# Projecting blocks 0 and 1 of a hybrid attention and expert layer one at a time, with new pacing marks

## What is computed

```python
h = rms_norm(x, norm1_w)
proj = einsum('bsd,dc->bsc', h, w_in)          # 3592 columns: q,k,v (8 heads of 64), conv q,k,v (4 of 128), gate, a, b
# group A: stick-breaking attention, a block of 128 queries against all earlier keys
# group B: causal conv of width 4 + silu, then a gated delta net whose state runs from block to block
mix = concatenate([o_sb, o_gdn]);  x = x + mix @ w_out
# PEER: for every token 8 heads x 16 experts out of 16384
q = (hn @ w_q); s1, s2 = scores against two sets of 128 sub keys; top 16 of each, top 16 of the sums -> experts, gates
act = gelu(einsum('thkd,td->thk', u_table[experts], hn)) * gates
out = x + einsum('thk,thkd->td', act, v_table[experts])
```

## Time and profile before

| | us |
|---|---|
| median of 3 runs | 3555.86 |
| lowest, highest | 3548.87, 3561.72 |
| the profiled execution, its own time | 3561.24 |
| its span, first to last instruction | 3559.5 |

### The profile page before, as it was taken

How to read it: one execution, slowest core, us unless ns; L and a number is a source line. 1 busy time by engine, 2 the same in 40 slices (tenths; PEclk the granted TensorE clock), 3 DMA queues, 4 the chain that set the end, 5 groups by cost and what they waited for, 6 DMA issues and landing times.

```text
span 3559.5 us, 46354 instructions
## 1 busy us (share of the span) xinstructions
PE 2354.7 (66%) x16193; PEld 1425.5 (40%) x16193; DVE 2318.2 (65%) x5421; ACT 849.8 (24%) x2344; POOL 2308.0 (65%) x2091
## 2 busy tenths in 40 slices
PE   7663546885847759767848859758847784344477
PEld 6543424653524436534524536534514451000011
DVE  3436887776697597666698587667696658444400
ACT  3330012331213223313114123314103311111122
POOL 1001775555667777677777677577687768777775
PEclk9887657897868879878869879878858885555555
DMA  7542899998989999999999999999999999999999
GB/s 233 190 169 97 312 356 328 351 374 301 349 321 357 410 373 411 412 381 390 409 374 387 409 384 410 368 389 395 406 371 369 407 409 346 387 409 409 409 403 374
DMA packets 398905, 1276.24 MB, mean 359 GB/s; under 512 B 44302, under 2 KB 99667, under 8 KB 389459
## 3 DMA queue, kind: packets, MB, share of 16 engines
q0 software_dynamic: 294912, 1073.87, 78.2%
q1 hardware_dynamic: 85330, 157.45, 12.2%
q10 hardware_dynamic: 18432, 41.95, 3.2%
HBM read 1232.18 MB, written 40.93 MB: 358 GB/s over the span
## 4 chain that ended last, share of the span: by engine, by line
POOL 25%; PE 24%; DVE 18%; DMA 17%; issue 9%; ACT 3%; DVEq 3%; ACTq 1%; SPq 0%; POOLq 0%
PE zz L1489 14%; POOL u_ring L684 13%; POOL v_ring L699 11%; DMA v_ring<-in_peer_v,idxT 9%; DVE u_ring L1067 5%; PE va L1489 4%; PE rr L1489 4%; DMA u_ring<-in_peer_u,idx 4%; DMA u_ring<-in_peer_v,idxT 2%; PE ox L1489 1%; DMA work<-d_w 1%; POOL u_ring L699 1%; DVE work L1398 1%; DVE work L1400 1%; DMA work<-d_gv 1%
## 5 line engine op out<-in xcount | busy, mean ns | idle before, releaser
L684 POOL DMA_INDIRECT u_ring<-in_peer_u,idx x1024 | 1177.2, 1150 | 786.4 <-DVE work L1414 330.3
L1067 DVE SCALAR_TENSOR_TENSOR u_ring<-u_ring,hn_t 128x1024 f32<-128x1024 f32 x1024 | 1223.1, 1222 | 387.2 <-DMA u_ring<-in_peer_u,idx 383.6
L699 POOL DMA_INDIRECT v_ring<-in_peer_v,idxT x960 | 1061.5, 1106 | 422.2 <-issue 248.6
L1489 PE MATMUL va<-v_ring,column 128*32 128x256 f32 x7680 | 748.3, 493 | 618.3 <-DMA v_ring<-in_peer_v,idxT 562.8
L1489 PE MATMUL zz<-work 128*128 128x256 f32 (+3 forms) x3232 | 739.0, 390 | 62.4 <-DVE work L1248 12.6
L1489 PEld LDWEIGHTS zz<-work 128*128 128x128 f32 (+1 forms) x3232 | 552.6, 212 | 270.7 <-issue 136.6
L1489 PEld LDWEIGHTS va<-v_ring,column 128*32 128x32 f32 x7680 | 196.9, 124 | 1096.9 <-DMA v_ring<-in_peer_v,idxT 888.0
L763 ACT ACTIVATE column<-onehot,wT 128x32 f32<-128x32 f32 x1024 | 285.9, 315 | 805.7 <-PE va L1489 777.5
L1489 PE MATMUL zz<-work,w_q_t 128*128 128x128 f32 x1024 | 132.0, 292 | 1.8 <-DVE work L1314 1.8
L1489 PEld LDWEIGHTS zz<-work,w_q_t 128*128 128x128 f32 x1024 | 127.1, 206 | 14.2 <-issue 11.5
L1489 PE MATMUL rr<-work,later 128*128 128x512 f32 x144 | 97.3, 796 | 40.0 <-DVE work L1267 31.1
(11 more groups left out here) (245 smaller groups left out, 2519.1 us busy)
## 6 DMA issues: line engine op xcount, KB each, us to landing
work<-d_w SPq DMA_DIRECT2D x42, 1024.0 KB, 8.5
work<-in_w_out ACTq DMA_DIRECT2D x64, 512.0 KB, 9.5
u_ring<-in_peer_u,idx POOLq DMA_INDIRECT x1024
v_ring<-in_peer_v,idxT POOLq DMA_INDIRECT x960, 10.4
work<-d_kT SPq DMA_DIRECT2D x36, 256.0 KB, 8.2
work<-d_v SPq DMA_DIRECT2D x36, 256.0 KB, 6.6
work<-in_x SPq DMA_DIRECT2D x16, 512.0 KB, 7.6
w_q_t<-in_peer_w_q SPq DMA_DIRECT2D x1, 8192.0 KB, 26.6
```

Source lines behind the costliest of these rows:

```text
L684: g.indirect_dma_start(u_ring[:, n % RU, :], None, u_rows, bass.IndirectOffsetOnAxis(idx[b % 2][:, s:s + 1], 0)).then_inc(u_landed[n % RU] ...
L699: g.indirect_dma_start(v_row(n), None, v_rows, bass.IndirectOffsetOnAxis(idxT[b % 3][:, t:t + 1], 0)).then_inc(v_landed[slot] if slot < RV ...
L1067: v.scalar_tensor_tensor(u_ring[:, m % RU, :], u_ring[:, m % RU, :], 1.0, hn_t[b % 2][:, :], ALU.mult, ALU.mult, accum_out=dots[:, s:s + 1 ...
L1489: return t_.matmul(out_, lhsT, rhs, start=start, stop=stop, skip_group_check=True)
```

## The change

The segments no longer have one size: `SIZES = (1, 1, 2, 2, 2)`, with `B0` their first blocks (0, 1, 2, 4, 6, 8). Blocks 0 and 1 are projected alone, with operands 128 wide instead of 256; blocks 2 to 7 are projected in pairs as before. There are five projections, and that of block 1 comes between `mixing(0)` and `mixing(1)`, where gathers of block 0 can run. All counters of semaphores that were `SEG * g` become `B0[g]`, and all tiles of `projection` are cut to `size * 128`. The points get 37 more steps with a weight of 3.5, and `MARKS` is a new table.

```diff
-SEG = 2
+SIZES = (1, 1, 2, 2, 2)
+B0 = [sum(SIZES[:g]) for g in range(len(SIZES) + 1)]
+SEG = max(SIZES)
...
 def segment_before(b):
-    return b // SEG if b >= 2 and b % SEG == 0 else None
+    return B0.index(b) if b and b in B0 else None
...
-                yield ("p", segment_before(b), n), 5.0 if n < NCH else 2.5, None if n < 4 or token_turn_pending(n) else 1
+                size = SIZES[segment_before(b)]
+                yield ("p", segment_before(b), n), (5.0 if size == 2 else 3.5) if n < NCH else 2.5, None if n < 4 or token_turn_pending(n) else 1
...
-MARKS = [(1, 0.62, 128, 0), (1, 1.0, 128, 40), (2, 1.0, 250, 118), (4, 1.0, 500, 368), (6, 1.0, 756, 624), (7, 1.0, 884, 750)]
+MARKS = [(1, 0.62, 128, 0), (1, 1.0, 128, 78), (2, 0.75, 256, 118), (2, 1.0, 256, 160), (3, 1.0, 364, 240), (4, 1.0, 503, 371), (6, 1.0, 758, 628), (7, 1.0, 886, 752)]
...
                 if g:
-                    sp.wait_ge(h_done, SEG * g)
-                for n in range(SEG):
-                    sp.dma_start(x_seg[:, n, :], x_blk[SEG * g + n]).then_inc(x_landed[n], 16)
+                    sp.wait_ge(h_done, B0[g])
+                for n in range(SIZES[g]):
+                    sp.dma_start(x_seg[:, n, :], x_blk[B0[g] + n]).then_inc(x_landed[n], 16)
...
-                            a.activation(s_ring[n % 7], mm_bank[n % 2], ACT.Copy).then_inc(evacuated, 1)
+                            a.activation(s_ring[n % 7][:, 0:w], mm_bank[n % 2][:, 0:w], ACT.Copy).then_inc(evacuated, 1)
...
-                            last = v.scalar_tensor_tensor(s_ring[n % 7], cb[c % 2][:, k:k + ST], vecs[:, w[k]:w[k] + 1],
-                                                          s_ring[n % 7], ALU.mult, ALU.add)
+                            last = v.scalar_tensor_tensor(s, cb[c % 2][:, k:k + w_t], vecs[:, w[k]:w[k] + 1], s, ALU.mult,
+                                                          ALU.add)
...
             def projection(g):
-                pe.wait_ge(xT_act, SEG * (g + 1))
+                pe.wait_ge(xT_act, B0[g + 1])
+                size = SIZES[g]
+                w = size * P
...
-                                last = mm(mm_bank[n % 2], wc[:, k, P * (n % 2):P * (n % 2) + P], xT[:, k, :], k == 0, k == KC - 1)
+                                last = mm(mm_bank[n % 2][:, 0:w], wc[:, k, half], xT[:, k, 0:w], k == 0, k == KC - 1)
```

More of the change, by code:

```diff
@@ L771, in x_squares @@
             def x_squares(g):
-                for n in range(SEG):
-                    act.wait_ge(x_landed[n], 16 * (g + 1))
+                for n in range(SIZES[g]):
+                    act.wait_ge(x_landed[n], 16 * sum(size > n for size in SIZES[:g + 1]))
                     if n:
@@ L781, in x_seeds @@
                 act.wait_ge(x_meaned, 2 * g + 1)
-                seed(y8, ms8, x_seeded)
+                seed(y8[:, 0:SIZES[g]], ms8[:, 0:SIZES[g]], x_seeded)
             def x_scale(g):
                 act.wait_ge(x_meaned, 2 * g + 2)
-                for n in range(SEG):
+                for n in range(SIZES[g]):
                     a.activation(x_seg[:, n, :], x_seg[:, n, :], ACT.Copy, scale=r8[:, n:n + 1]).then_inc(x_scaled, 1)
@@ L791, in x_copies @@
                     act.wait_ge(vecs_ready, 2)
-                for n in range(SEG):
-                    act.wait_ge(x_turned, SEG * g + n + 1)
+                for n in range(SIZES[g]):
+                    act.wait_ge(x_turned, B0[g] + n + 1)
                     for k in range(KC):
@@ L1518, in x_turns @@
             def x_turns(g):
-                for n in range(SEG):
-                    pe.wait_ge(x_scaled, SEG * g + n + 1)
+                for n in range(SIZES[g]):
+                    pe.wait_ge(x_scaled, B0[g] + n + 1)
                     turn((rr if n else zz)[:, :], x_seg[:, n, :], KC).then_inc(x_turned, 1)
             def projection(g):
-                pe.wait_ge(xT_act, SEG * (g + 1))
+                pe.wait_ge(xT_act, B0[g + 1])
+                size = SIZES[g]
+                w = size * P
                 for n in range(NCH + 9):
@@ L1533, in projection @@
                         for k in range(KC):
[L1534 to L1535 removed]
+                            half = slice(P * (n % 2), P * (n % 2) + P)
+                            if kind in "az" and size == 2:
+                                last = mm(mm_bank[n % 2], xT[:, k, half], wc[:, k, :], k == 0, k == KC - 1)
+                            elif kind in "az":
+                                last = mm(mm_bank[n % 2][:, 0:w], xT[:, k, 0:w], wc[:, k, half], k == 0, k == KC - 1)
                             else:
[L1537 removed]
+                                last = mm(mm_bank[n % 2][:, 0:w], wc[:, k, half], xT[:, k, 0:w], k == 0, k == KC - 1)
                         last.then_inc(projected, 1)
@@ L1559, in projection @@
                         weights_read()
-                        for p in range(SEG):
+                        for p in range(size):
                             for k in range(KC):
```

114 lines of the change are left out of this document (61 added, 53 removed).

## The result

The changed kernel takes 3621.34 us, median of 4 runs (3614.24 to 3624.36), against 3555.51 us (3548.87 to 3561.72) of the kernel before: 1.0182 times the time, 95% interval 1.0162 to 1.0202. I had forecast 3541 us. It is 66 us slower, and the prediction was wrong in sign and size.

A forecast was written before the change was run, and what follows sets the result against it. It took the time as the start of gathers plus bytes behind it over the rate, with transfers binding from 1050 us. Terms: 1822 us to block 4's numbers + 1174 + 549 = 3545, median about 3541; range 3505 to 3574.

The forecast's parts named there:

- The start: Up to the first gather: half-width projection(0) takes 105 us instead of 148, moving the first gather from 340 to 294 us.
- Projection(1): Block 1's new separate projection, behind the first gather: 170 us (146 to 211), with 77 dots on VectorE.
- The rival that made this stage the culprit: Projection(1) held by ACT and DVE's back and forth with dots between: 211 us, end 41 us later, 3582; chance 0.13.
- Block 1's mixing: Mixing of block 1 with 51 U and 65 V rows: 205 us, against 300 with 168 gathers before.
- Blocks 2 to 4: the marks: Blocks 2 to 4 by the new table's rows: 415, 290 and 448 us, block 4's numbers at 1822 us.
- Block 3: Block 3, with 188 instead of 178 planned rows: 290 us (280 to 300).
- block 4: Block 4, with 270 instead of 322 rows: 448 us, between 432 if transfers bind and 470 if work does.
- blocks 5 to 7: From block 4's to block 7's numbers, plan the same within two rows: 1174 us.
- the tail: Last stretch, only gathers, 410 instead of 414 rows: 549 us, 5 less than 554.
- The account of 46 us earlier against 45 us of bytes: First gather 46 us earlier, against 18 MB more moved behind it, 45 us at 401 GB/s.
- The gain must come from the rate: Start's gain and added bytes about cancel (46 and 45 us), so any gain needs a higher transfer rate behind the first gather.
- The bytes take it all: Rival for the whole kernel: 46 us earlier and 45 us more traffic cancel, time stays at 3556; chance 0.25.

The follow-up runs named there:

- the last set: Runs on one chip with weights copied HBM to HBM under block 0's mixing: changed kernel with the marks of before 3583.33 us, kernel before 3558.97, unmodified 3556.82.
- the late copy: Changed kernel with the marks of before, weights copied HBM to HBM under block 0's mixing instead of stored in projection(0): 3583.33 us, 1.0081 of the kernel before.
- The half dots: Changed kernel with block 0's dots over columns 0 to 511 of 1024, gathers whole, scores incomplete: 3867.83 us, 1.0135 of the kernel before.
- the last pair: Weights copied HBM to HBM under block 0's mixing, in the changed kernel with the marks of before (1.0081) and in the kernel before (1.0006).

## Why the prediction was wrong

**The start: right mechanism, a size off.** "I take 105 us (bounds 85 and 125), since weights and stores must then run at four fifths of what the DMAs can do." It was 125, its own upper bound, at share 0.72. Without the stores it was 104 us, so the back and forth of ACT and DVE did shrink as worked out, and the stores held the rest: 22 us of the error. I had the bytes' busy time as one bound and the halved work as the other, and took their larger with a margin. Near each other, the two terms added here: VectorE waits for its own small stores behind megabytes.

**Projection(1): right.** 164 us for 170, at 351 GB/s; it moved 84 gathers, where I had counted 77 dots. The rival that made this stage the culprit, at 211 us, was not what happened. The kernel got slower with this stage as forecast, and that rival's price (41 us) was too small for the result besides. The prediction had named this stage as the place where it would go wrong most of all; it went wrong in the next.

**Block 1's mixing: the step that failed.** "The nearest row is block 2's mixing, 213 us ...; the floor is block 0's, 175 us with none. I take 205 us." It took 244, 39 us more, which alone turns the 14 us of gain into a loss. Rows of the kernel before would have come near it. The floor of 175 us was itself 8 too long, since its stretch begins at 165 us and block 0's mixing at 172.8 (the first instruction of L1183). What failed is the cost of the 116 rows: I put them at 30 us over the floor, and they took 77. Block 1's mixing took 299 us with 169 gathers, block 0's about 167 with none (91 and 75 for its two parts in the last set, or up to 93 and 76), so each gather beside this work added 0.78 us. The 110 gathers issued make 86, and 167 and 86 are 253, 9 too many. Split by part, with the last two sets of windows: the first part has a floor of 91 to 93 us, and adds 0.91 us a gather in the kernel before (200 with 119) and 0.88 here (143 with 57). Much of that lies in the dots, 1.22 us each on VectorE: they stand in the chain rather than beside it. The chain of waits of the changed kernel, 480 to 624 us, by line and with two of its pieces (start, length):

```profile
by line: DVE u_ring L1075 28.6%; PE zz L1504 20.9%; DMA work<-d_gv 7.6%; PE ox L1504 6.3%; PE rr L1504 3.8%; issue 2.9%; ACTq L881 2.1%; PE va L1504 2.0%; DVE work L1297 1.9%; DVE work L1253 1.8%; PE rr L1508 1.4%; DVE work L1279 1.3%; DVE 
...
487.44 4.65 DVE u_ring L1075 x7
...
511.52 4.58 DVE u_ring L1075 x8
```

And the chain by line of the same part of block 0's mixing, 119 to 212 us of the changed kernel with the late copy, where there are no dots:

```profile
by line: PE zz L1502 39.6%; PE ox L1502 7.2%; PE rr L1502 7.2%; ACTq L879 4.1%; ACT work L901 3.3%; issue 3.0%; PE rr L1506 2.1%; DVE work L1298 1.5%; DVE work L1280 1.5%; DVE work L1295 1.5%; DVE work L1325 1.3%; ACT work L948 1.2%; DVE st
```

Dots stand three or four together between the steps of the delta net, 29% of the chain, and its small steps wait behind them. They are 41 us of 144, and the stage is 51 us longer than block 0's 93; TensorE's pieces sum to 50 us here and 53 there. The half dots show the limit of this: VectorE had 26 us less to do, which at 0.88 of 1.22 would be 19 us of stage, and the stage lost 8. So the cost of a row is shown as a price, and the dot as a part of it, with transfers close behind. The kernel before pays it too; but there the rows covered the stage with transfers, 119 of 0.524 MB in 200 us at share 0.92. The new structure takes 85 U rows in projection(1), and then the mixing has its own floor of 167 us with few rows left to fill it. The floors say it shortly: ahead of block 1's numbers there stand 167 us of work in the old kernel and 167 + 104 in the new one (104 is what projection(0) took without the stores), with the same 168 rows to cover them under the marks of before. 168 rows are 222 us of transfers at 1.32.

**Blocks 2 to 4: the marks.** "Share 0.92 leaves room for most of the 9 to 23 more: 415 us." 225 gathers were issued in 434 us, 11 more than the 214 before for 23 us more. The projection of the stage did fill up (0.98 at 372 GB/s), but it was planned so full of U rows that none was left for the last 87 us (0.80), a place that the prediction did not look at. The experiments put the marks at 20 us. Block 3, block 4 (455 for 448), blocks 5 to 7 and the tail were right within 9 us each.

**The ledger.** Three parts come out of the ratios. The structure costs 0.8% (1.0081 with the copy moved and old marks). The copy's hold on projection(0) costs about 0.5% (1.0135 less 1.0081). The marks cost 0.5%. They sum to 1.9%, against 1.82% measured, or 29, 19 and 18 us of 3556. The middle one is the least sure, since its two intervals overlap and come from different chips; the 26 us at the first gather support it. The account of 46 us earlier against 45 us of bytes fits the last pair (48 and 41) as far as it goes. What it lacked was the idle transfer time that a stage moved behind the first gather brings with it. My sentence "The gain must come from the rate" named the open point; the rate fell there instead.

**Of the rivals**, none was the case. "The bytes take it all" is nearest, in its account for the start. The Trainium skill (DMA: Bandwidth & Descriptors, Where 436 GB/s comes from) gives 358 GB/s as a core's half of the memory's rate. The trace did not bear it out as a limit for this core on this chip (395 in the tail). In the other sets the tail runs at 355 to 361, which would fit it, but no run shows whether another core was at work there; the ratio of the two kernels is the same within the intervals (1.0182, 1.0202, 1.0223).

**Open.** Which of VectorE, POOL and the transfers would bind projection(1) alone: each was within some 10 us of the others. How most of the time that bytes cost in projection(1) is taken back later. How much TensorE's low clock costs in block 1's mixing. Whether the sizes (1, 2, 2, 2, 1) gain with marks that fit them. No kernel that does the whole computation was faster here than the one before by an amount that a measurement can tell, so there is no better version to show.

## What to carry to other kernels

When work moves from ahead of the first transfer to behind it, price it twice: the bytes it adds, and the length by which the stage now outlasts the transfers that are there to cover it. Price a stage with rows beside it as its floor without rows plus a cost for each row, both read from stages of the kernel itself, rather than from the nearest stage in name. And when marks take rows early, ask which stretch behind goes without.

## What was unexpected of the hardware

A dot of 128x1024 on VectorE (1222 ns, two inputs in SBUF) lengthens the gathers issued beside it: 1333 ns a gather with full dots, 986 with half ones on the same chip, and 1250 against 1028 in projection(1). A copy of 14.7 MB within HBM, put into the first part of block 0's mixing, made its 93 us 0.91 busy at 322 GB/s, and that part is 91 to 92 us long without it. Filling TensorE raised its granted clock from 0.67 to 0.84 and the stage took 8 us longer, with the filling in its chain. And the same tail of the changed kernel had 395 GB/s in one set and 356 and 359 in two others, a tenth apart.
